# ScalarE copies the turned probabilities of unit n - 3 before, not after, the exponential of unit n

## The chip, the cores and the metric

The kernel runs on one core of a Trainium2 chip. The metric is the device time of one execution in microseconds (us), lower is better. The engines are called by their names in the profile: PE (TensorE matmul), PEld (TensorE weight load), DVE (VectorE), ACT (ScalarE), POOL (GpSimd), SP (SyncE, which here only issues DMAs).

## The reference, cut to what matters

A first block (a convolution and latent-attention mixer, then a mixture of 32 experts) and a second block of two layers run over 512 tokens of width 1024, in f32. Only the attention of the second block's layers is touched by the change. Each layer has two kinds of heads, eight of each:

```python
# kind "a": window of the own and the previous block of 128 keys, with a sink
s = jnp.where(mask, qk * D ** -0.5, NEG)
m = jnp.maximum(s.max(-1, keepdims=True), sink)
pr = jnp.exp(s - m)
denom = pr.sum(-1, keepdims=True) + jnp.exp(sink - m)
o = (pr / denom) @ vv
# kind "b": the same without a sink, over the 128 keys that an index score selects
```

## The kernel before

The attention of a layer is cut into 64 **units** (list `UNITS`, line 61): one unit is one head `h` of one block `t` of 128 queries of one kind. The order is a1, a2, a3 (24 units, 256 keys wide each), b1 (8 units, 256 wide), b2 (8, 384 wide), b3 (8, 512 wide), b0 (8, 128 wide), a0 (8, 128 wide). The whole is run twice, once for each layer, by a loop in the program (`Fori(0, LAYERS)`), so there are 128 units in an execution.

A unit goes through these steps, each with the line that the profile shows:

- PE writes the scores into one of four banks, `bank=n % 4` (L2098), and adds the mask (L2105, L2108, L2109). The scores of two units are made together, at even n.
- DVE takes the row maximum (L1680) and negates it into the bias (L1682 for kind a, L1685 for kind b). This is the signal `y_neg`.
- ACT takes the exponential out of the bank into `Pr2` (L1182). This frees the score bank.
- PE turns the probabilities (L2117, a matmul with the identity) into bank 4 or 5.
- ACT copies them to `PT2` (L1173), which has three buffers. This frees the bank.
- PE multiplies them with the values (L2128) into the bank of the output of eight units (6 or 7).
- After eight units DVE divides by the sum (L1696, L1697) and takes the output out of its bank (L1699, `take_o`).

The order on each engine is written out by hand as a software pipeline over n. PE, at step n: the scores of n and n + 1 if n is even, the turn of unit n - 3, the values of unit n - 4, and at n = 19 to 23 the turn of one more block of keys or queries (L2033, bank 7). DVE, at step n: the row maximum of n, at 21 of the steps 7 to 37 one pick (L1654 and L1655: the next eight largest index scores), and at n = 11, 19, 27 and so on the `take_o` of the eight units that end with n - 4. ACT, at step n, before the change: it waits for the maximum of unit n, takes the exponential of unit n, then copies the turned probabilities of unit n - 3; at n = 19 to 23 it also takes the extra turned block out of bank 7 (L1105).

The engines run their instructions in the order written, and wait on semaphores: `Use.begin` waits until a bank is free, `Use.read` until it is full, `Use.evacuated` until a named content of a bank has been taken out. The scores of n and n + 1 (n even) need the exponentials of n - 4 and n - 3; the turn of n - 3 needs the exponential of n - 3; the values of n - 4 need the copy of n - 4. On ACT the exponential of n also waits until the copy of n - 4 is complete (by then PE has read the `Pr2` buffer that the exponential writes to), and the copy of n - 3 waits for the values of n - 6.

After the 64 units PE turns the outputs (L2033, keys `oT`) and multiplies with `w_o` (L2156). The load of `w_pg` is issued by SP when the first `oT` bank is full (L806).

Of the kernel before, what the change touches and what calls it, by code (L numbers as in the profile page):

```python
# [235 lines left out]
def build(nc, i, out, stop=None):  # L236
    ctx = ExitStack()
    with ctx:
# [451 lines left out]
        def width(n):  # L690

            kind, t, h = UNITS[n]
            return min(t + 1, 2) * P if kind == "a" else (t + 1) * P

        def weighted2(eng, n, l):

            kind, t, h = UNITS[n]
            if h == 7:
                u2.read(eng, ("o", kind, t), l)
            else:  # L700
                y_pv.wait(eng, l, n - n // 8 + 1)
# [250 lines left out]
        def _(act):  # L952
# [59 lines left out]
            n = 0  # L1012
# [83 lines left out]
            with act.Fori(0, LAYERS) as l:  # L1096
                own.restart()
                def take_in(t, j):
                    a, b = IN_CUTS[j]
                    ps = u2.read(act, ("in", t, j), l)  # L1100
                    u2.free(act.copy(PJ[:, t, a:b], ps[:, 0:b - a]), ("in", t, j))

                def take_turned(key, dst):
                    ps = u2.read(act, key, l)
                    u2.free(act.copy(dst, ps[:]), key)  # L1105
# [41 lines left out]
                n = 0  # L1147
# [19 lines left out]
                def take_pt(n):  # L1167
                    kind, t, h = UNITS[n]
                    w = width(n)
                    if n >= 3:  # L1170
                        weighted2(act, n - 3, l)
                    ps = u2.read(act, ("pT", kind, t, h), l)
                    u2.free(act.copy(PT2[:, n % 3, 0:w], ps[:, 0:w]), ("pT", kind, t, h))  # L1173

                for n, (kind, t, h) in enumerate(UNITS):
                    w = width(n)
                    kk = 0 if kind == "a" else 1
                    y_neg.wait(act, l, n + 1)
                    if n >= 4:
                        u2.evacuated(act, ("pT",) + UNITS[n - 4], l)  # L1180
                    ps = u2.read(act, ("s", kind, t, h), l)
                    u2.free(act.activation(Pr2[:, n % 4, 0:w], ps[:, 0:w], ACT.Exp, bias=nmx2[:, kk, t, h:h + 1],  # L1182
                                           scale=HD ** -0.5, accum_out=ls2[:, kk, t, h:h + 1]), ("s", kind, t, h))
                    if n < T - 2:
                        take_in(n + 2, 4)
                    if n >= 3:
                        take_pt(n - 3)
                    if n in TURN_AT:
                        key = TURNED[TURN_AT[n]]
                        take_turned(key, turned[key])  # L1190
                    if kind == "a" and h == 7:
                        y_sinkd.wait(act, l, WINDOWED.index(t) + 1)
                        y_sinke.inc(act.activation(es2[:, t], es2[:, t], ACT.Exp))
# [18 lines left out]
                n = 0  # L1212
# [1017 lines left out]
```

How the kernel before makes its waits and increments, by code:

```python
    def settle(self):  # L101
        self.eng.wait_ge(self.sem, self.n)
# [421 lines left out]
            def begin(self, pe, key, i=0):  # L524
                n, u = self.b.where[key]
                if self.b.before[n] + u > 0:
                    pe.wait_ge(bank_free[n], self.b.before[n] + u + i * self.b.uses[n])
                return bank[n]
# [4 lines left out]
            def read(self, eng, key, i=0):  # L533
                n, u = self.b.where[key]
                eng.wait_ge(bank_full[n], self.b.before[n] + u + 1 + i * self.b.uses[n])
                return bank[n]
# [4 lines left out]
            def evacuated(self, eng, key, i=0):  # L541
                n, u = self.b.where[key]
                eng.wait_ge(bank_free[n], self.b.before[n] + u + 1 + i * self.b.uses[n])
# [19 lines left out]
            def wait(self, eng, layer, k):  # L563
                eng.wait_ge(self.sem, layer * self.per + k)
# [138 lines left out]
        def down_loaded(eng, f, l):  # L703
            per = (FC - 1 - f % DN_SLOTS) // DN_SLOTS + 1
            eng.wait_ge(d_dn[f % DN_SLOTS], 16 * per * l + 16 * (f // DN_SLOTS + 1))
# [1 line left out]
        @block.sync  # L708
# [30 lines left out]
            u1.read(sp, ("oT", 0))  # L739
            load_expert(2, 2)
            u1.read(sp, ("mix", T - 1, 1))
            load_expert(0, 0)
            load_expert(1, 1)
            sp.wait_ge(s_x1, T)
            sp.wait_ge(s_slots, 16 * (2 * T))
            sp.dma_start(slots_f, slot_table.rearrange("(q p) o -> q (p o)", p=P)).then_inc(s_slotin, 16)
            for n in range(4):
                sp.wait_ge(m_st[n], SCATTERED)
            for g in range(2):
                for q in range(T):
```

## Time and profile before

| | us |
|---|---|
| median of 3 runs (lowest, highest) | 2382.17 (2379.54, 2385.83) |
| the profiled execution, own time | 2389.93 |
| span of its trace | 2388.2 |
| PE busy | 2117.3 (89%) |
| DVE busy | 962.7 (40%) |
| ACT busy | 595.8 (25%) |
| mean granted TensorE clock | 0.93 |

The span runs from the first to the last instruction; 1.7 us lie around it. The attention of the first layer stands at about 992 to 1122 us of the span, that of the second at about 1741 to 1871 us. A matmul's end is modelled in this profile, so that neighbouring matmuls overlap a little: what a piece of work takes is best read from start to start. In brackets behind an instruction stands how long its engine had been idle before it, and which instruction ended that.

### The profile page before, as it was taken

How to read it: one execution, taken by the hardware profiler on the slowest of the kernel's cores; microseconds unless marked ns; L12 is line 12 of the kernel's file. 1: busy time of each engine (PE TensorE's matmuls, PEld its weight loads, DVE VectorE, ACT ScalarE, POOL GpSimd, SP SyncE). 2: the span in 40 equal slices, each digit the busy share in tenths (PEclk: the TensorE clock that was granted, in tenths of full speed). 3: DMA queues.
4: the chain of work that ended last, by engine and by line, in shares of the span. 5: the costliest groups of instructions: out<-in, count | busy, mean ns of one | idle time of the engine just before them, and what ended most of it. 6: DMA issues, size and time to landing. Idle time of an engine off the chain costs nothing. (4 is left out here: it accounts for less than half of the span.)

```text
span 2388.2 us, 24926 instructions
## 1 busy us (share of the span) xinstructions
PE 2117.3 (89%) x8645; PEld 1435.0 (60%) x8645; DVE 962.7 (40%) x1735; ACT 595.8 (25%) x1122; POOL 112.9 (5%) x175
## 2 busy tenths in 40 slices
PE   3986788379999959889999999998989999999995
PEld 1542544344444435677478887885567657888784
DVE  1554952221111156772523222334866242222335
ACT  1121321011111112244223332221244222333221
POOL 2000000201011010000100000001000000000001
PEclk7996999589999978988999999999899899999998
DMA  8307012258877561001103334224000211333320
GB/s 271 118 0 277 7 54 89 90 209 313 322 303 304 217 237 42 1 19 71 62 18 89 104 88 140 80 89 145 1 1 19 97 53 36 105 88 112 109 97 35
DMA packets 154638, 269.43 MB, mean 113 GB/s; under 512 B 12225, under 2 KB 109681, under 8 KB 141361
## 3 DMA queue, kind: packets, MB, share of 16 engines
q1 hardware_dynamic: 147696, 258.46, 30.8%
q0 software_dynamic: 6848, 9.77, 1.4%
q8 instruction: 53, 0.87, 0.1%
q14 instruction: 41, 0.33, 0.0%
HBM read 257.64 MB, written 23.14 MB: 118 GB/s over the span
## 5 line engine op out<-in xcount | busy, mean ns | idle before, releaser
L231 PE MATMUL bank<-ht_hi,gate_up_hi 128*128 128x512 f32 x704 | 274.1, 389 | 2.9 <-ACT arena L1218 2.9
L232 PE MATMUL bank<-ht_lo,gate_up_hi 128*128 128x512 f32 x704 | 273.9, 389 | 0.0
L233 PE MATMUL bank<-ht_hi,gate_up_lo 128*128 128x512 f32 x704 | 273.9, 389 | 0.0
L1985 PE MATMUL bank<-arena 128*128 128x512 f32 x512 | 226.9, 596 | 3.7 <-DVE arena L1527 3.7
L2045 PE MATMUL bank<-arena 128*128 128x512 f32 (+3 forms) x640 | 199.1, 473 | 8.1 <-ACT arena L1111 7.4
L2045 PEld LDWEIGHTS bank<-arena 128*128 128x128 f32 x640 | 118.6, 203 | 85.6 <-issue 74.7
L1985 PEld LDWEIGHTS bank<-arena 128*128 128x128 f32 x512 | 95.6, 192 | 112.2 <-issue 108.2
L231 PEld LDWEIGHTS bank<-ht_hi,gate_up_hi 128*128 128x128 f32 x704 | 132.2, 188 | 31.2 <-issue 3.8
L233 PEld LDWEIGHTS bank<-ht_hi,gate_up_lo 128*128 128x128 f32 x704 | 132.2, 188 | 27.6
L232 PEld LDWEIGHTS bank<-ht_lo,gate_up_hi 128*128 128x128 f32 x704 | 132.2, 188 | 27.1
L231 PE MATMUL bank<-down_hi,product_hi 128*128 128x512 f32 x352 | 138.2, 392 | 3.5 <-DVE arena L1732 3.5
L1732 DVE TENSOR_TENSOR arena<-arena,bank 128x512 f32 (+1 forms) x44 | 30.3, 688 | 272.1 <-ACT arena L1130 272.1
L233 PE MATMUL bank<-down_hi,product_lo 128*128 128x512 f32 x352 | 138.1, 392 | 0.0
L232 PE MATMUL bank<-down_lo,product_hi 128*128 128x512 f32 x352 | 138.0, 392 | 0.0
L1726 DVE TENSOR_TENSOR gate_up_lo<-gate_up_whole,gate_up_hi 128x2048 fp32r<-128x2048 f32 x44 | 100.9, 2292 | 67.3 <-ACT gate_up_hi L1124 66.7
L1736 DVE TENSOR_TENSOR down_lo<-down_whole,down_hi 128x1024 fp32r<-128x1024 f32 x44 | 53.9, 1225 | 157.6 <-ACT product_hi L1138 157.6
L2001 PE MATMUL bank<-arena 128*128 128x512 f32 x256 | 115.2, 592 | 0.7 <-ACT arena L1069 0.7
L2156 PE MATMUL bank<-arena 128*128 128x512 f32 x256 | 111.1, 593 | 1.7 <-ACT arena L1105 1.7
L2128 PE MATMUL bank<-arena 128*128 128x64 f32 x544 | 88.7, 292 | 20.4 <-ACT arena L1173 19.8
L1532 DVE TENSOR_TENSOR arena<-arena,bank 128x256 f32<-128x256 f32 x32 | 13.5, 421 | 220.8 <-ACT arena L1064 220.8
L1825 PE MATMUL bank<-arena 128*128 128x128 f32 (+1 forms) x301 | 48.8, 315 | 57.6 <-DMA arena<-slot_table 28.3
L2128 PEld LDWEIGHTS bank<-arena 128*128 128x128 f32 x544 | 79.0, 210 | 29.5 <-ACT arena L1173 28.3
(319 smaller groups left out, 3088.4 us busy)
## 6 DMA issues: line engine op xcount, KB each, us to landing
gate_up_whole<-w_gu SPq DMA_DIRECT2D x88, 512.0 KB, 5.0
arena<-w_gate_e SPq DMA_DIRECT2D x32, 1024.0 KB, 4.9
arena<-w_up_e SPq DMA_DIRECT2D x32, 1024.0 KB, 7.6
arena<-w_down_e SPq DMA_DIRECT2D x32, 1024.0 KB, 9.7
arena<-w_ada SPq DMA_DIRECT2D x12, 2048.0 KB, 12.2
down_whole<-w_down SPq DMA_DIRECT2D x44, 512.0 KB, 3.5
arena<-w_in SPq DMA_DIRECT2D x4, 2048.0 KB, 14.8
arena<-w_o SPq DMA_DIRECT2D x2, 4096.0 KB, 14.1
```

The costliest lines, as they stand in the source:

```text
L231: pe.matmul(ps, xh, wh, start=start, stop=False)
L232: pe.matmul(ps, xh, wl, start=False, stop=False)
L233: return pe.matmul(ps, xl, wh, start=False, stop=stop)
L1726: dve.tensor_tensor(gu_lo[s], gu[s], gu_hi[s].bitcast(F32), ALU.subtract).then_inc(f_lo, 1)
L1732: dve.tensor_tensor(dst, SF[:, s], bank[2 * s + 1][:], ALU.mult).then_inc(f_a, 1)
L1736: dve.tensor_tensor(dn_lo[f % 2], w_dn[:, f % DN_SLOTS], dn_hi[f % 2].bitcast(F32), ALU.subtract)
L1825: ins = pe.transpose(ps[0:x.shape[-1], n * P:(n + 1) * P], x, ident)
L1985: ins = pe.matmul(bank[s % 2][:], XW[s % 2][:, c], ring[s][:, :, c], start=c == 0, stop=c == C8 - 1)
L2001: ins = pe.matmul(bank[4 + 2 * (s % 2) + half][:], AT[:, s % 2, c], ring_d[s][:, c, 512 * half:512 * half + 512], start=c == 0, stop=c == 1)
L2045: ins = pe.matmul(ps[:, 0:b - a], HT[:, c, t * P:(t + 1) * P], w_in2[j][:, c], start=c == 0, stop=c == C8 - 1)
L2128: ins = pe.matmul(ps[:, h * HD:(h + 1) * HD], PT2[:, n % 3, k * P:(k + 1) * P], v, start=k == 0, stop=k == nk - 1)
L2156: ins = pe.matmul(ps[:], HT[:, m, t * P:(t + 1) * P], w_o2[:, m, 512 * half:512 * half + 512], start=m == 0, stop=m == C8 - 1)
```

## The change

ACT's two operations of step n change places: the copy of the turned probabilities of unit n - 3 is issued first, then the wait for the maximum of unit n and its exponential. Nothing is added or removed, and no other engine's program is touched.

```diff
                 for n, (kind, t, h) in enumerate(UNITS):
                     w = width(n)
                     kk = 0 if kind == "a" else 1
+                    if n >= 3:
+                        take_pt(n - 3)
                     y_neg.wait(act, l, n + 1)
                     if n >= 4:
                         u2.evacuated(act, ("pT",) + UNITS[n - 4], l)
@@
                                            scale=HD ** -0.5, accum_out=ls2[:, kk, t, h:h + 1]), ("s", kind, t, h))
                     if n < T - 2:
                         take_in(n + 2, 4)
-                    if n >= 3:
-                        take_pt(n - 3)
                     if n in TURN_AT:
                         key = TURNED[TURN_AT[n]]
                         take_turned(key, turned[key])
```

## Rows read from the trace of the kernel before

**Rows 1.** The page: engines, then the costliest groups (busy, mean ns, idle before, releaser)

```profile
PE 2117.3 (89%) x8645; PEld 1435.0 (60%) x8645; DVE 962.7 (40%) x1735; ACT 595.8 (25%) x1122; POOL 112.9 (5%) x175
...
L2128 PEld LDWEIGHTS bank<-arena 128*128 128x128 f32 x544 | 79.0, 210 | 29.5 <-ACT arena L1173 28.3
```

**Rows 2.** Windows of the first layer: us, each engine's busy time, PEclk, DMA share, GB/s

```profile
1009.00:1070.00 61.00, 51.83 (x351) 41.68 (x348) 47.64 (x130) 27.21 (x92) 0.00 (x0) 0.89 0.06 19
1072.00:1100.00 28.00, 27.99 (x213) 23.55 (x212) 9.26 (x29) 14.23 (x38) 0.00 (x0) 0.97 0.00 1
1100.00:1122.00 22.00, 18.92 (x119) 16.03 (x118) 8.00 (x32) 9.59 (x46) 0.00 (x0) 0.75 0.01 1
```

**Rows 3.** Timeline around units 8 to 14 (start us, us, engine, line; idle in brackets)

```profile
1008.11 0.70 PE L2098 MATMUL bank<-arena 64*128 64x256 f32 x4
...
1010.73 0.52 PEld L2128 LDWEIGHTS bank<-arena 128*128 128x128 f32 x4 [0.39 <-ACT arena L1173]
...
1011.32 0.70 PE L2098 MATMUL bank<-arena 64*128 64x256 f32 x4
...
1013.43 0.69 DVE L1699 TENSOR_TENSOR arena<-bank,arena 128x512 f32<-128x512 f32 x1
1014.04 0.41 DVE L1680 TENSOR_REDUCE arena<-bank 128x1 f32<-128x256 f32 x1
...
1014.82 0.47 ACT L1182 ACTIVATE arena<-bank,arena 128x256 f32<-128x256 f32 x1 [2.22 <-DVE arena L1682]
...
1015.28 0.36 ACT L1173 COPY arena<-bank 128x256 f32<-128x256 f32 x1
1015.70 0.93 PEld L2128 LDWEIGHTS bank<-arena 128*128 128x128 f32 x4 [2.01 <-ACT arena L1173]
1015.70 1.12 PE L2128 MATMUL bank<-arena 128*128 128x64 f32 x4 [1.82 <-ACT arena L1173]
...
1016.74 1.23 PE L2098 MATMUL bank<-arena 64*128 64x256 f32 x4
...
1021.85 1.23 PE L2098 MATMUL bank<-arena 64*128 64x256 f32 x4
```

**Rows 4.** Waits, 1009 to 1070 us: who for whom, us in total, times, longest

```profile
DVE arena L1680 <- PE bank L2109: 7.9, 5, 2.1
...
DVE arena L1680 <- PE bank L2105: 2.2, 3, 0.9
```

**Rows 5.** Waits, 1757 to 1818 us (second layer; its L2105 row reads as in rows 4)

```profile
DVE arena L1680 <- PE bank L2109: 7.0, 5, 2.8
```

**Rows 6.** Timeline: the extra turn at n = 19 in the first layer

```profile
1031.02 0.69 DVE L1699 TENSOR_TENSOR arena<-bank,arena 128x512 f32<-128x512 f32 x1
...
1031.77 0.66 PE L2033 MATMUL bank<-arena 128*128 128x128 f32 x4 [1.72 <-DVE arena L1699]
...
1033.78 0.43 DVE L1680 TENSOR_REDUCE arena<-bank 128x1 f32<-128x256 f32 x1 [2.06 <-PE bank L2109]
```

**Rows 7.** Timeline of narrow units, first layer: score pairs, one unit's ACT work, the end

```profile
1101.90 0.49 PE L2098 MATMUL bank<-arena 64*128 64x128 f32 x4
...
1104.23 0.49 PE L2098 MATMUL bank<-arena 64*128 64x128 f32 x4
...
1106.18 0.30 PEld L2128 LDWEIGHTS bank<-arena 128*128 128x128 f32 x2 [0.71 <-ACT arena L1173]
1106.18 0.43 PE L2128 MATMUL bank<-arena 128*128 128x64 f32 x2 [0.52 <-ACT arena L1173]
1106.30 0.37 ACT L1182 ACTIVATE arena<-bank,arena 128x128 f32<-128x128 f32 x1 [0.17 <-ACT arena L1173]
1106.55 0.30 PEld L2098 LDWEIGHTS bank<-arena 64*128 64x128 f32 x4
...
1111.45 0.80 PE L2098 MATMUL bank<-arena 64*128 64x128 f32 x4
...
1113.83 0.50 PEld L2128 LDWEIGHTS bank<-arena 128*128 128x128 f32 x2 [0.16 <-ACT arena L1173]
...
1114.45 0.80 PE L2098 MATMUL bank<-arena 64*128 64x128 f32 x4
...
1121.65 5.20 PE L2033 MATMUL bank<-arena 128*128 128x128 f32 x32 [0.79 <-DVE arena L1699]
```

**Rows 8.** Timeline of narrow score pairs, second layer

```profile
1850.37 0.49 PE L2098 MATMUL bank<-arena 64*128 64x128 f32 x4
1852.70 0.49 PE L2098 MATMUL bank<-arena 64*128 64x128 f32 x4
1855.02 0.67 PE L2098 MATMUL bank<-arena 64*128 64x128 f32 x4
...
1863.88 0.80 PE L2098 MATMUL bank<-arena 64*128 64x128 f32 x4
```

## The prediction, made before the changed kernel was run

> **What bounds the kernel now.** I read the page first. PE is busy for 89% of the span [rows 1], and one wait on it belongs to this change: the weight loads of the values, L2128, stood idle 28.3 us for the copy of the turned probabilities, L1173, over both layers [rows 1]. I count this on PEld, because the matmul rows start later and hide part of the same gap (in the worst place 1.82 us on PE, 2.01 us on PEld [rows 3]). Outside the two attention stretches the change touches nothing, so 28.3 us plus what the clock gives back is all there is.
>
> Then the windows, since a stage with 128-wide units has other limits than one with 512-wide ones [rows 2]. Three regimes show. From 1009 to 1070 us, where DVE also makes its picks, DVE is busy 47.64 of 61 us and PE 51.83: neither is full and both wait for each other. From 1072 to 1100 us (384 and 512 wide) PE is full, 27.99 of 28 us: nothing to gain. From 1100 to 1122 us (128 wide) PE waits again, DVE and ACT are under half busy, and the clock is 0.75.
>
> The timeline shows the loop behind the waits [rows 3]. PE issues the scores of a pair, the turn and the values of the units before, one more turn, and then wants the values of unit n - 4 at odd n. These need the copy, and the copy stands on ACT behind the exponential of unit n - 1, whose scores PE made in this very pair. So PE waits for scores, maximum (0.41 us), exponential (0.47), copy (0.36): at 1013.43 us DVE is busy with an output, the maximum comes at 1014.04, the exponential at 1014.82, the copy at 1015.28, the values at 1015.70 after 2.01 us. Right then the clock falls to its lower level, 1.2 GHz: the next score pairs start 5.11 us apart (1016.74 to 1021.85), before it 3.21 us apart (1008.11 to 1011.32).
>
> **The change part by part.** The copy of n - 3 no longer waits for the exponential of n. No instruction is added or removed, and no DMA moves except with the end of the stage. ACT's work stays 27.21 us in a stretch of 61 [rows 2], so its sum is no limit.
>
> *What the removed wait gives.* The values of n - 4 now need the exponential of n - 2 instead of n - 1. At odd n that is one of the pair before, finished long ago. The stall of the pair goes.
>
> *What is late next.* The exponential of n now stands behind the turn of n - 3, and is due at the turn of n, three steps on, or at the scores of n + 3. Between the turn of n - 3 and that of n lie three steps, at 3.21 us per two steps some 4.8 us; the copy (0.36), the exponential with its accumulator read (0.46, from its start to that of the copy [rows 3]) and the semaphores need under 1.5 us, and at 128 wide three steps are at least 2.5 us. I cost this at nothing; if the cover were gone it would cost the copy's time per pair (a rival, below). One small thing improves: the exponential of n waits until the copy of n - 4 is complete, which now ended a whole unit earlier, so the bubble of 0.17 us behind the copy [rows 7] goes. It lies beside PE's work: nothing.
>
> *First term, the units without picks (n below 8).* Stalls of up to 0.39 us per pair as in the row at 1010.73 [rows 3], three pairs a layer, PE otherwise full: 1 us a layer, **2 us**.
>
> *Second term, the stretch with picks.* Here PE can only gain what DVE lets it. DVE's idle time for PE is 7.9 + 2.2 = 10.1 us in the first layer [rows 4] and 7.0 + 2.2 = 9.2 in the second [rows 4, 5], 19.3 together: with DVE full, that is the most the stretch can shrink, though PE would gain more with its waits gone and the clock up. Part of it stays: at n = 19 PE's extra turn waits 1.72 us for the output that DVE takes from bank 7, and the next scores stand behind it, so DVE idles 2.06 us afterwards [rows 6]. The same place in the second layer is inside the longest wait of 2.8 [rows 5]. That is about 4.9 us untouched; 14.4 remain. The bounds are 0 and 14.4. I take somewhat over half, **8 us**, because DVE also waits for PE at each output, and PE, no longer blocked, still meets a DVE that holds it back.
>
> *Third term, the 128-wide units.* At the full clock, pairs are 1106.55 - 1104.23 = 2.32 us apart with 0.52 us (PE) to 0.71 (PEld) of stall; without it about 1.75. At the lower clock 1114.45 - 1111.45 = 3.00 us with 0.16 of stall, 2.84 without [rows 7]. If the clock falls where it does now, four pairs of the first layer gain 0.57 each and the last 0.16, in the second layer two and three (from 1850.37, 1855.02 and 1863.88 [rows 8]): 2.4 + 1.6 = 4.0 us. If it stays up, the five pairs go from 12.55 us (1101.90 to 1114.45) to 8.75 and from 13.51 to 8.75, 8.6 us together, and the end of the stage, 1114.45 to 1121.65 us, 7.2 us at the lower clock in each layer, has the turns and values of some four units and no scores; I count them as one and a half pairs, which lose 2.84 - 1.75 = 1.09 us each, so up to 1.6 us a layer (an estimate): 11.8 us. Between 4.0 and 11.8 I take **8 us**, since fewer stalls speak for a clock that holds, and these matmuls are the thinnest of the stage.
>
> The Trainium skill, "TensorE: Matmul & The Clock Gate", section "A second HAM failure mode: psum-queue depth-cycling", says that small idle times between groups of matmuls make the clock go up and down even where none is long. The trace agrees: it fell after 2.01 us of idle at 1015.7 us, and in the narrow units after stalls of 0.71 (the scores' rows grow from 0.49 to 0.80 us in [rows 7] and [rows 8]). By that rule alone this term would be at its upper end, 11.8 us, and the whole 22 us.
>
> Sum: 2 + 8 + 8 = **18 us** off. What follows the stage is bound to it (SP loads after the first turned output, PE goes straight on), so the gain is not given back. The profiled execution takes 2389.9 us and would take 2371.9. It lies 7.8 us above the median of the runs shown; against the median the forecast is 2382.2 - 18 = **2364 us**, 0.76% less.
>
> **The rivals.**
>
> *DVE is the bound.* For: it is busy 78% of the stretch with picks, its chained operations leave gaps that the busy share does not count, and the loss at n = 19 shows who leads. Then the second term is 0, the stalls only move to the turn, and the clock falls as before: 2 + 4 = 6 us, 2376. Against: DVE did stand idle for PE for 19.3 us. The Trainium skill, "Perfetto Trace Analysis", section "Identifying the Most-Contended Engine", would have one optimize the most-contended engine first, which in that stretch by its measures (DVE's occupancy over PEld's) is DVE, and this change gives DVE nothing; by it this rival is right.
>
> *The clock holds throughout.* All upper ends: 2 + 14.4 + 11.8 = 28 us, 2354. For: both kinds of fall in the stage stand beside stalls of this wait. Against: the wait at n = 19 stays, and the clock fell behind it too.
>
> *Slower: the late exponential.* ACT now waits at the head of its queue for the turn of n - 3 while the maximum of n is ready. If PE reaches the scores of n + 3 or the turn of n before that exponential, every pair in the stretch with picks pays about one copy, 0.36 us: 2 layers x 16 pairs x 0.36 = 11.5 us slower, 2394. It decides only once less than 0.4 us of the slack above is left; the rows give some 3 us at 256 wide and 1 us at 128 wide.
>
> *The change does nothing.* The values of n - 4 could be held by something else that ends with the same copy. Against: the copy starts within 0.1 us of the end of the exponential and its read [rows 3], not of a matmul. 2382.
>
> **How the numbers follow.** Chances: forecast 0.60 (a gain of 12 to 24 us), DVE the bound 0.18, the clock holds 0.11, nothing 0.06, slower 0.05. The range for 8 in 10 takes the forecast and the larger part of its two neighbours: 2354 to 2377. A measurement of this kernel can tell about 0.3%, 7 us, from no change. Faster by more: the forecast, the clock case and a third of DVE the bound, 0.60 + 0.11 + 0.07 = 0.78. Same: 0.17. Slower: 0.05.
>
> **What would show it right or wrong.** L2128's wait for L1173, 28.3 us now, should fall under 8; the maximum L1680's waits for PE in the stretch with picks from 19.3 to about 11. Narrow score pairs should stand about 1.75 us apart at the full clock. The wait of L2033 at n = 19 should stay. The forecast is wrong if the idle time turns up at the turn L2117 waiting for the exponential L1182 (then DVE, or the late exponential, is the bound), or if the pairs close up and the granted clock falls lower than 0.75 in the narrow units.

## The result, and the profile after

The changed kernel takes 2352.17 us (median of 4 runs, 2352.06 to 2356.39); the kernel before takes 2382.14 us (4 runs, 2379.54 to 2385.83). The ratio is 0.9877, 95% interval 0.986 to 0.9894: 30 us less. The direction was forecast, the size was not: 18 us were named, the range ended at 2354, and the time of the rival "the clock holds throughout", 2354 us, is the nearest.

The weight loads of the values still wait for the copy, but less. In the groups by line, where 28.3 us stood [rows 1]:

```profile
L2128 PEld LDWEIGHTS bank<-arena 128*128 128x128 f32 x544 | 71.7, 193 | 12.6 <-ACT arena L1173 12.0
```

16 us of this wait are gone, and 30 us of the time. The windows show what else changed (us; busy time of PE, PEld, DVE, ACT and POOL; granted clock PEclk; DMA share; GB/s; the first layer with picks, mostly 512 wide, 128 wide):

```profile
1000.00:1060.00 60.00, 52.47 (x403) 42.95 (x399) 50.75 (x140) 29.38 (x101) 0.00 (x0) 0.94 0.06 19
1060.00:1084.00 24.00, 24.00 (x186) 19.77 (x184) 9.43 (x27) 13.31 (x35) 0.00 (x0) 1.00 0.00 1
1084.00:1106.00 22.00, 19.94 (x161) 17.08 (x160) 8.77 (x36) 13.60 (x54) 0.00 (x0) 1.00 0.12 39
```

Against [rows 2] DVE is now fuller beside its picks (50.75 of 60 us, was 47.64 of 61), and the clock in the narrow stretch is 1.00 where it was 0.75. The last window even has room for the turn of the outputs, which before lay behind it. The narrow score pairs, in the timeline of the changed kernel (start, us, engine, line):

```profile
1089.07 0.49 PE L2098 MATMUL bank<-arena 64*128 64x128 f32 x4
...
1090.15 0.27 ACT L1173 COPY arena<-bank 128x128 f32<-128x128 f32 x1 [0.57 <-PE bank L2117]
1090.47 0.43 PE L2128 MATMUL bank<-arena 128*128 128x64 f32 x2
...
1090.83 0.49 PE L2098 MATMUL bank<-arena 64*128 64x128 f32 x4
...
1096.12 0.49 PE L2098 MATMUL bank<-arena 64*128 64x128 f32 x4
...
1101.08 3.71 PE L2033 MATMUL bank<-arena 128*128 128x128 f32 x32 [0.78 <-DVE arena L1699]
1101.77 4.01 ACT L1105 COPY arena<-bank 128x512 f32<-128x512 f32 x8 [1.96 <-PE bank L2033]
1105.84 0.70 PE L2156 MATMUL bank<-arena 128*128 128x512 f32 x1 [1.05 <-ACT arena L1105]
```

The pairs stand 1.76 us apart, and the copy now waits for the turn (L2117), as the new order has it. Beside [rows 7]: a pair took 2.32 to 3.00 us, the end from the last scores to the turn of the outputs 7.2 us (now 4.96), and that turn's 32 matmuls 5.20 us (now 3.71).

One wait grew. At n = 19, where PE waited 1.72 us [rows 6]:

```profile
1021.97 0.69 DVE L1699 TENSOR_TENSOR arena<-bank,arena 128x512 f32<-128x512 f32 x1
1022.71 0.71 PEld L2033 LDWEIGHTS bank<-arena 128*128 128x128 f32 x4 [4.09 <-DVE arena L1699]
1022.71 1.11 PE L2033 MATMUL bank<-arena 128*128 128x128 f32 x4 [3.95 <-DVE arena L1699]
...
1025.35 0.42 DVE L1680 TENSOR_REDUCE arena<-bank 128x1 f32<-128x256 f32 x1 [2.69 <-PE bank L2109]
...
1030.31 0.42 DVE L1680 TENSOR_REDUCE arena<-bank 128x1 f32<-128x256 f32 x1 [2.19 <-PE bank L2109]
```

PE comes earlier and DVE, bound by its own work, does not, so PE waits 3.95 us, and at this wait stands the one fall of the clock left in the stage (1.11 us for a turn that takes 0.66 at the full clock). DVE's two waits, for the scores of n = 20 and of n = 22, stand behind it.

**Where the time went, by steps.** From the starts of the score pairs (first row of each pair on PE), in us. The profile of the kernel before was taken twice (the second time as an experiment, below). "wo" is the first matmul with `w_o`.

| steps | before, layers 1, 2 | before again, 1, 2 | changed, 1, 2 |
|---|---|---|---|
| 6 to 20 | 30.68, 28.15 | 28.08, 30.67 | 26.85, 26.85 |
| 20 to 40 | 42.57, 42.01 | 42.16, 42.58 | 36.74, 36.89 |
| 40 to 52 | 26.97, 26.97 | 26.97, 26.97 | 26.81, 26.82 |
| 52 to 62 | 12.55, 13.51 | 11.78, 12.40 | 8.81, 8.81 |
| 62 to the outputs' turn | 7.20, 7.20 | 7.09, 7.19 | 4.96, 4.96 |
| outputs' turn to wo | 6.09, 6.71 | 6.19, 6.22 | 4.76, 4.76 |

The means of steps 6 to wo are 124.7 us before and 109.0 after: 15.7 us a layer. Steps 0 to 6 add 0.6 each in the profiles. That is some 33 us, against 30 in the medians. The two profiled spans differ by 37.8 us (2388.2 and 2350.4); step 6 was reached at 1001.68 us in the one and 996.91 in the other, of which the program's first 987 us, the same in both kernels, give 4.2. In the eleven profiles of this study step 6 of the first layer stands between 994.3 and 1001.7 us: that is mostly scatter of the first block.

### The profile page after: what moved, and what is told of

It is laid out like the page before. It is cut to its first block, busy times and chain, and to the rows that moved or that the text cites. A ratio compares the mean times of both kernels' runs of the same rounds, so it can differ in the third digit from the quotient of the medians.

```text
span 2350.4 us, 24926 instructions
## 1 busy us (share of the span) xinstructions
PE 2091.1 (89%) x8645; PEld 1411.8 (60%) x8645; DVE 961.3 (41%) x1735; ACT 593.3 (25%) x1122; POOL 112.8 (5%) x175
## 4 chain that ended last, share of the span: by engine, by line
PE 76%; DVE 13%; DMA 4%; issue 3%; POOL 2%; ACT 2%; SPq 0%; DVEq 0%; ACTq 0%; POOLq 0%
PE bank L231 11%; PE bank L233 11%; PE bank L232 11%; PE bank L1985 9%; PE bank L2156 5%; PE bank L2001 5%; PE bank L2045 4%; PE bank L1942 2%; PE bank L1849 2%; DVE arena L1655 2%; DMA arena<-w_ada 2%; PE bank L2117 2%; DVE arena L1654 2%; PE bank L2128 2%; PE bank L2098 1%
## 5 line engine op out<-in xcount | busy, mean ns | idle before, releaser
L2045 PEld LDWEIGHTS bank<-arena 128*128 128x128 f32 x640 | 119.3, 205 | 86.4 <-issue 75.6
L1985 PEld LDWEIGHTS bank<-arena 128*128 128x128 f32 x512 | 95.6, 192 | 112.2 <-issue 108.3
L1803 PE MATMUL bank<-arena 128*32 128x512 f32 x192 | 37.0, 915 | 64.2 <-DMA arena<-w_ada 64.1
L1295 DVE SCALAR_TENSOR_TENSOR arena<-arena 128x512 f32<-128x512 f32 x120 | 89.9, 749 | 3.1
```

The source lines that it names most:

```text
L1295: ins = dve.scalar_tensor_tensor(DW[:, m], U[:, m, k:k + S], conv_w[:, m, k:k + 1], DW[:, m], ALU.mult, ALU.add)
L1985: ins = pe.matmul(bank[s % 2][:], XW[s % 2][:, c], ring[s][:, :, c], start=c == 0, stop=c == C8 - 1)
L2045: ins = pe.matmul(ps[:, 0:b - a], HT[:, c, t * P:(t + 1) * P], w_in2[j][:, c], start=c == 0, stop=c == C8 - 1)
```

## The experiments

Eight kernels were timed in 4 to 6 runs each beside the kernel before, and one was profiled only; the medians of the kernel before in the three sessions were 2383.88, 2382.98 and 2380.50 us.

**The kernel before, once more.** No edit.

> The kernel before, profiled once more, to see how much its stages move between executions. If the clock's falls at 1015, 1032, 1070 and 1111 us belong to the stalls there, they stand at the same units again, and the two attention stages (first scores to first matmul with w_o) are within 3 us of the first profile's 136.0 us in the first layer. If the clock falls by luck, a stage moves by 5 us or more, and a part of the 37.8 us between the two profiled spans is luck.

2385.29 us, span 2383.6. The stages are in the table above. Neither outcome came clean: the stretch 6 to 20 moved between 28.1 and 30.7 us (the clock fell at unit 12 in the first layer of the one execution and in the second of the other), while the 20 to 40 stretch and the narrow units repeat within 2 us. Steps 6 to wo took 122.3 us in place of 126.1 in the first layer, 3.8 us less, between the 3 us named for the one case and the 5 us named for the other. So some 2.6 us a fall are luck, and a comparison must use more than one profile.

**The new order for a part of the units.** Both with this edit, the condition being `n < 40` or `n >= 40`:

```diff
+                    copy_first = n < 40
+                    if n >= 3 and copy_first:
+                        take_pt(n - 3)
                     y_neg.wait(act, l, n + 1)
...
+                    if n >= 3 and not copy_first:
+                        take_pt(n - 3)
```

> The new order for units 0 to 39 only (all the units beside which DVE makes its picks), the old one for 40 to 63. Theory (each stage gains by itself): the first 40 units gain 10.2 us in the first layer and 7.0 in the second, the narrow units nothing: 2382 - 17 = 2365 us. Rival (DVE is the bound beside the picks, and the gain comes from the narrow units and the clock there): 2376 us or more. Rival (the late exponential costs something that the narrow units pay back): 2382 or more.

2364.52 us against 2383.88, ratio 0.9914 (0.9894 to 0.9933): 19 us. Steps 6 to 40 took 63.8 and 63.6 us, as in the changed kernel. The rival that DVE bounds this stretch is out.

> The new order for units 40 to 63 only. Theory (each stage gains by itself): the narrow score pairs stand 1.76 us apart and the clock holds there, 7.5 us in the first layer and 9.0 in the second: 2382 - 16 = 2366 us. Rival (the clock in the narrow units holds only because the units before it also ran without stalls): the pairs close up to about 1.8 but fall to 2.8 as the clock falls, 4 us in all: 2378 us.

2370.11 us, ratio 0.9944 (0.9924 to 0.9964): 14 us. Steps 52 to 62 took 8.81 us in both layers, the rest of the stage 9.73. Steps 6 to 40 kept the old 70.2 us with their stalls, and the clock held in the narrow units all the same (PEclk 1.00 from 1094 to 1116 us):

```profile
1094.00:1116.00 22.00, 19.94 (x156) 16.79 (x155) 8.48 (x35) 13.63 (x54) 0.00 (x0) 1.00 0.12 38
```

So the clock there depends on what PE does there, and the two parts add: 19 + 14 = 33 us, beside 30.

The run with `n < 40` gives one thing more. Its narrow units have the old order, and in its second layer the clock happened to hold (timeline, PE; in this kernel L2101 are the scores and L2131 the values):

```profile
1838.02 0.49 PE L2101 MATMUL bank<-arena 64*128 64x128 f32 x4
1840.03 0.43 PE L2131 MATMUL bank<-arena 128*128 128x64 f32 x2 [0.57 <-ACT arena L1173]
1840.39 0.49 PE L2101 MATMUL bank<-arena 64*128 64x128 f32 x4
```

There the old order took 11.78 us for steps 52 to 62, 5.57 to the outputs' turn and 4.76 to wo, 22.1 in all. The new order takes 18.5; the old one with a fall of the clock took 26.0 on average in the four passages of the table. So of 7.5 us a layer, 3.6 are the removed wait and 3.9 are the clock, by the one passage in which it held. It fell in five of these six passages of the old order (once only behind the last score pair), and between steps 52 and 62 in none of the fourteen passages of the new order in this study. Behind them, in the turn of the outputs, it did fall in two of the fourteen (the first layers of the last two runs below).

**DVE takes the output before its pick.** In the changed kernel:

```diff
+                    if n >= 4 and (n - 3) % 8 == 0:
+                        take_o(*UNITS[n - 4][:2])
                     if n in PICK_AT:
                         pick(PICKS_C + PICK_AT.index(n))
-                    if n >= 4 and (n - 3) % 8 == 0:
-                        take_o(*UNITS[n - 4][:2])
```

> The changed kernel, and DVE takes a finished output (take_o) before the pick of the same step, not behind it. Theory (at n = 19 PE waits 3.9 us for DVE, which is late by its own work): the pick of 1.6 us moves behind the output, the wait of L2033 falls from 3.9 to about 2.3 us, and the kernel to 2352 - 3 = 2349 us, perhaps 2 us more if the clock holds behind it. Rival (DVE is the bound of the whole stretch, so that what it does first makes no difference): 2352 us.

2345.73 us against 2383.88, ratio 0.9843 (0.9823 to 0.9863). Beside the changed kernel's 0.9877 that is 6 us better by the medians and 8 by the ratios, with intervals that overlap; the rows show the step. The wait at n = 19 fell by the pick's 1.6 us:

```profile
1018.49 0.71 PEld L2033 LDWEIGHTS bank<-arena 128*128 128x128 f32 x4 [2.50 <-DVE arena L1699]
1018.49 1.12 PE L2033 MATMUL bank<-arena 128*128 128x128 f32 x4 [2.36 <-DVE arena L1699]
```

and steps 6 to wo from 108.9 and 109.1 us to 108.0 and 106.5, 3.5 together. The clock still fell behind it.

**One more ACT copy, in either order.** In the changed kernel between the copy and the exponential, in the kernel before between the exponential and the copy:

```diff
                     if n >= 3:
                         take_pt(n - 3)
+                        act.copy(R[:, (n % 3 + 1) // 2, 256 * ((n % 3 + 1) % 2):][:, 0:256], R[:, 0, 0:256])
                     y_neg.wait(act, l, n + 1)
```

> The changed kernel with one more ACT copy (128x256 f32, within SBUF, into a spare buffer, 61 a layer) between the copy of the turned probabilities and the exponential: it delays every exponential by about 0.36 us and nothing else. Theory (the exponential has microseconds of slack behind the copy): 2352 us, at most 5 us more, from the places where DVE is late. Rival (the late exponential is on the path and the change's gain is net of that cost): one copy per pair, 2 x 30 x 0.36 = 22 us more, 2374 us.

2353.53 us, ratio 0.9878 (0.986 to 0.9896): the same as the changed kernel's 0.9877, though ACT did 50.7 us more; only the end of the stage, behind the last scores, took 0.5 us more a layer:

```profile
L1180 ACT COPY arena<-arena 128x256 f32<-128x256 f32 x122 | 50.7, 415 | 0.0
```

> The kernel before with the same extra ACT copy between the exponential and the copy of the turned probabilities: it lengthens the chain from the scores to the values by about 0.36 us. Theory (in the old order this chain sets the pair's time wherever PE is not full, 25 of 32 pairs a layer): 2383 + 2 x 25 x 0.36 = 2401 us, and more where the clock falls more often. Rival (the copy was held by DVE's own work, so ACT has room): 2383 to 2388 us.

2399.66 us against 2382.98, ratio 1.007 (1.0053 to 1.0087): 17 us slower. The values' wait rose from 28.3 to 38.4 us, and the narrow steps 52 to 62 from 12.6 us to 15.4 and 14.9:

```profile
L2129 PEld LDWEIGHTS bank<-arena 128*128 128x128 f32 x544 | 80.3, 213 | 39.5 <-ACT arena L1173 38.4 <-issue 0.6
```

The same instruction costs nothing in front of the exponential and 17 us in front of the copy. That settles the rival of the late exponential. In units 40 to 63 the extra copy did delay it: from the end of its maximum's negation to its start it took 0.31 to 0.33 us longer on average than in the changed kernel, and the score pairs stood no further apart, so there the slack is at least that. In units 8 to 39 the delay was 0.10 us on average, since ACT mostly stands idle there for the maximum; the copy ran in that idle time, and how much slack the exponential has there is not shown.

**The picks spread evenly.** On top of the output before the pick:

```diff
-PICK_AT = [n for n in range(6, 38) if n % 3]
+PICK_AT = [n for n in range(38) if n % 9 in (1, 3, 5, 7, 8)]
```

> The kernel with the output before the pick (2345.7 us), and DVE's 21 picks at steps 1 to 37 spread evenly (1, 3, 5, 7, 8 of every nine) in place of two of three from step 7. Theory (with the new order DVE's own work bounds steps 14 to 40): four picks of 1.6 us a layer move to where DVE is idle: 2 x 6 = 12 us less, 2334 us. Rival (PE's remaining wait at n = 19 and its 2.75 us per pair bound the stretch): 2343 us or more.

2345.96 us, ratio 0.9844 (0.9825 to 0.9863): no gain that the medians show, and not the 12 us expected. By the rows, steps 20 to 40 fell from 37.4 and 36.4 us to 34.5 and 32.9, but steps 8 to 12 rose from 5.50 us to 8.26, where the picks meet the rotation of the keys that DVE makes at n = 5. Steps 6 to wo are 3.9 us less over both layers; the execution's first block was 4.1 us later. The clock was low for 3.4 us of steps 6 to 40, in the first layer alone, and before for 6.8 and 3.4 us, so part of the 3.9 us is the clock. With the later turn, in the two runs below, the same spread is worth 1.0 us over both layers (208.4 us for steps 6 to wo against 209.4).

**The extra turns behind the next scores.** On top of that, PE:

```diff
+                    if n - 1 in TURN_AT:
+                        turn_heads([TURNED[TURN_AT[n - 1]]])
                     if n < T - 2:
                         project(n + 2, 4)
...
-                    if n in TURN_AT:
-                        turn_heads([TURNED[TURN_AT[n]]])
```

> As the run with spread picks, and PE makes the extra turns of steps 19 to 23 one step later, behind that step's scores. Theory (the scores of units 20 and 21 stood behind PE's wait for bank 7, and DVE idled 2.7 us for them): 2 to 4 us less than the run with spread picks, 2331 us. Rival (DVE is full there anyway, or the later turn delays the b heads): no change or slower, 2334 us or more.

2342.09 us against 2382.98, ratio 0.9831 (0.9813 to 0.9848); one of its six runs took 4352 us, for no reason that was found (the median of the other five is 2340.71). The pair at n = 18 fell from 5.76 us to 2.74. It is the best kernel run here: 41 us under the kernel before, about 10 under the changed one.

> The kernel with the output before the pick and the extra turns one step later, but the picks where they were. Theory (the turn behind the scores gives 3 us in steps 6 to 20 of each layer as in the run with spread picks, and spreading the picks gives about 2 us a layer by itself): steps 6 to 20 in about 23 us, 2346 - 4 = 2342 us, within noise of the 2342.1 with spread picks. Rival (the two only work together, as DVE is too late at n = 19 with the picks where they were): 2346 us.

2345.48 us against 2380.50, ratio 0.985 (0.983 to 0.987). Steps 6 to 20 took 21.8 us in both layers, 3.0 to 3.5 less than with the output before the pick alone, so the later turn works without the spread; steps 6 to wo are 5.2 us less over both layers. DVE's two waits for the scores of n = 20 and 22 are gone: the view of the waits lists none of L1680 between steps 8 and 40 in either layer. In this run and the one before it the granted clock stayed full through all the units of both layers. In the first layer it then fell in the turn of the outputs, which took 5.38 us in place of 3.71:

```profile
1096.91 5.38 PE L2033 MATMUL bank<-arena 128*128 128x128 f32 x32 [0.78 <-DVE arena L1699]
```

The medians' intervals do not separate this run from the two before it.

## Why the prediction was wrong

**The mechanism was right.** The values waited for the exponential of a unit whose scores PE had just made, and the new order takes it out: the extra copy shows it from both sides, and the two halves of the change add up. The slack of the exponential, costed at nothing, costs nothing. Steps 40 to 52 (512 wide, and the first 128 wide ones) gained 0.15 us a layer (forecast nothing), and steps 0 to 8 gained 1.0 us a layer, the first term.

**The second term was mis-sized: 8 us forecast, 12 to 15 measured.** Steps 8 to 40 shrank by 9.2 and 6.0 us in the profiled pair (run with `n < 40`: 19 us with the first term). Some 3 of the 9.2 are luck, the fall of the clock at unit 12 that the profiled execution had in its first layer: of the six passages of the old order (the kernel before twice, and the run with the new order from 40 on) two took 70.0 us with that fall and four 66.9 to 67.0 without it, and the changed kernel took 60.8 and 61.0. The second layer's 6.0 us came with the clock low for 6.8 us before and 6.8 after.

Three steps of its working failed. It set too much aside and then halved the rest. Over steps 8 to 40 the view lists 11.4 and 9.5 us of DVE's waits for PE before the change and 4.9 and 5.0 after it. What is left are the two waits behind n = 19, for the scores of n = 20 and n = 22, and nothing else; every other listed wait went. The term set 4.9 us aside, and took the second layer's 2.8 us for the place of rows 6; it is the wait at n = 22, and beside it stands one at n = 20 (before the change, second layer):

```profile
1782.98 0.43 DVE L1680 TENSOR_REDUCE arena<-bank 128x1 f32<-128x256 f32 x1 [2.69 <-PE bank L2109]
...
1788.52 0.42 DVE L1680 TENSOR_REDUCE arena<-bank 128x1 f32<-128x256 f32 x1 [2.77 <-PE bank L2109]
```

Second, "somewhat over half" was a choice without a row: of the waits elsewhere, 11.4 us, all went. Third, the 19.3 us are the waits that the view lists between 1009 and 1070 and between 1757 and 1818 us; the stretch is longer (20.9 us are listed between steps 8 and 40), and the list is not all of DVE's idle time, so 14.4 us were no upper bound. From 1756.45 to 1823.40 us DVE was idle for 66.95 - 52.08 = 14.9 us and the list has 9.5. After the change, over the same units, 61.0 - 51.6 = 9.4 are left, 5.0 of them listed:

```profile
1756.45:1823.40 66.95, 56.78 (x408) 45.33 (x407) 52.08 (x142) 30.85 (x107) 0.00 (x0) 0.95 0.05 17
```

```profile
1733.20:1794.19 60.99, 53.46 (x407) 43.85 (x407) 51.59 (x141) 29.81 (x102) 0.00 (x0) 0.94 0.06 19
```

Over both layers of the profiled pair that makes 11.0 us from listed waits, 3.2 from idle time that the list leaves out and 1.0 from DVE's busy time, 15.2 in all. Once PE is no longer blocked, the waits that the view lists for DVE are those where the scores come late for another reason, and there was one such place left, n = 19; the later turn removed them too.

**The third term was mis-sized: 8 us forecast, 15 measured (14 in its own run), above its upper end of 11.8.** The 1.75 us per pair at the full clock came out as 1.76. But the middle was taken between "the clock falls as before" and "the clock holds", and the runs show no passage of the new order in between: it held from step 52 to 62 in all fourteen. The five pairs gained 7.5 us over both layers (12.56 to 8.81 us, means). The end of the stage gained 4.4 where 3.2 was the most, since it also loses waits for the copy (0.6 us a layer, 5.57 to 4.96 at the full clock). And the turn of the outputs behind it, 3.1 us, was not counted at all: its 32 matmuls ran at the clock that the narrow units left them.

**The rivals.** "The clock holds throughout" got a chance of 0.11 and was nearly right with 28 us: the clock did fall once more, at n = 19, and the terms that were too small covered it. The argument for it, that the falls stood beside stalls of this wait, was in the rows, and the text then weighed it less than the wait at n = 19. "DVE is the bound" is refuted as put (6 us): DVE was given nothing, and the stretch beside its picks shrank by 11%. An engine with 78% occupancy was not the bound while the other engine waited on it in turns. What the prediction drew from the Trainium skill's rule in "Perfetto Trace Analysis", section "Identifying the Most-Contended Engine", is refuted with it. The rule itself names what to optimize first, and that the runs do not refute: moving DVE's own work gave some 6 us more. The Trainium skill's rule on small idle times in "TensorE: Matmul & The Clock Gate", section "A second HAM failure mode: psum-queue depth-cycling", fits the narrow units: the old order's stall of 0.5 to 0.8 us per pair went with a fall in five passages of six. One passage had the same stalls and held, so the stalls alone do not decide. By that rule alone the term was at its upper end, the better forecast.

**What was named to look for.** The wait of L2128 was to fall under 8 us; it fell to 12.0, since PE still meets DVE's lateness beside the picks (most at n = 14 and 16, 0.56 and 1.12 us on PE). The maximum's waits for PE were to fall from 19.3 us to about 11; over steps 8 to 40 they fell from 20.9 to 9.9. No idle time turned up at the turn L2117 waiting for the exponential. The wait at n = 19 was to stay; it grew by 2.2 us on PE, because its other side is DVE's time.

## What to carry to other kernels

When a wait sits in a ring of engines none of which is full, moving one instruction to use the older of two operands can free all of them at once, and what it is worth is bounded by the idle time of each engine (window length less busy time), not by the waits that a view lists. Where stalls are regular and the clock is seen at both levels, treat it as two cases, each with its own chance and full price, and follow it into the work behind the stretch. To see whether an operation has slack, put a known one in front of it: the same copy cost nothing in one place and 17 us in the other.

## What the runs showed of the hardware

The clock's falls in the old order were partly luck. At unit 12, behind the same chain of waits, it fell in one layer and not in the other, the other way round in the second execution (30.7 and 28.1 us for steps 6 to 20), and in neither layer of the run with the new order from 40 on (27.95 and 28.12). In the changed kernel both layers repeat within 0.2 us per stretch; with DVE's work moved they did not always (steps 20 to 40: 37.4 and 36.4 us, and with the picks spread 34.5 and 32.9). In the narrow units no single stall was longer than 0.8 us when it fell; without the stalls it held from step 52 to 62 in all fourteen passages. It could fall even behind these: in the two runs with the later turn it had been full since the stage began, and in the first layer fell 0.5 us into the turn of the outputs, behind an idle time of 0.78 us on PE.

The clock rises again while PE does nothing but transposes. In seven passages of the old order (two of them with the extra copy) the clock was low when the outputs' turn (L2033) began, and each time the rise falls inside it. What PE did before the turn may have had a part in it; no run takes that away. In the kernel before, PE makes nothing but this turn from 1121.65 to 1126.85 us, and the granted clock goes from 1.2 to 2.4 GHz inside it (windows of 1 us: us, PE busy, PEclk, DMA share, GB/s):

```profile
1123.00:1124.00 1.00, 1.00 (x6) 0.50 0.00 0
1124.00:1125.00 1.00, 1.00 (x8) 0.63 0.71 37
1125.00:1126.00 1.00, 1.00 (x11) 1.00 0.92 329
```
